# Token-wise queries, keys and values for cross attention, and a state space block in two parts around the normed output's transposes

## The reference

```
def gated_rmsnorm(y, z, w):                       # after each group's scan
    u = y * silu(z); ug = u in 8 groups of 256
    return ug * rsqrt(mean(ug * ug) + EPS) * w

def memory_cross_attention(h, mem_n, ...):
    q = rmsnorm_2((h @ wq_x).reshape(S, 4, 128), xq_norm_g)
    kv = (mem_n @ wkv_x).reshape(256, 2, 4, 128)
    k = rmsnorm_2(kv[:, 0], xk_norm_g); v = kv[:, 1]
    p = softmax(q k^T * 128 ** -0.5)
    return (p v).reshape(S, 512) @ wo_x
```

## Time and profile before

| | |
|---|---|
| median of 3 runs | 1980.33 us (1977.35 to 1981.42) |
| the profiled execution's own time | 1978.49 us |
| its span | 1976.8 us |
| state space stage | about 97 to 481 us of the span, some 50 us a group |
| cross attention, first key panel to first scores | 1491.3 to 1562.97 us |
| PE busy | 96% of the span |

### The profile page before, as it was taken

The page is one execution under the profiler, slowest core; times in us unless marked ns, Lnnn a source line. Parts: engine busy times, 40 slices in busy tenths (PEclk is TensorE's granted clock), DMA queues, the critical chain, the costliest instruction groups (busy, mean ns, idle before and its releaser), DMA issues.

```text
span 1976.8 us, 26607 instructions
## 1 busy us (share of the span) xinstructions
PE 1900.3 (96%) x9819; PEld 1601.9 (81%) x9819; DVE 851.5 (43%) x1696; ACT 712.0 (36%) x1334; POOL 1458.1 (74%) x1307
## 2 busy tenths in 40 slices
PE   6999999999999999989999999898999989999998
PEld 4888888887887888878888888797678878888887
DVE  3666666663004443545501421637661354302411
ACT  4466666655014665123101210467643332101200
POOL 6799888789865446988988988653436358888984
PEclk9999999999999999989999999899999899999999
DMA  7322122222342222322333233222023112333331
GB/s 212 97 61 63 59 63 65 64 65 64 107 123 65 75 60 86 129 85 64 106 86 106 85 107 88 71 71 65 30 66 129 54 42 87 100 92 100 91 107 64
DMA packets 213069, 165.71 MB, mean 84 GB/s; under 512 B 14446, under 2 KB 209329, under 8 KB 212578
## 3 DMA queue, kind: packets, MB, share of 16 engines
q1 hardware_dynamic: 207286, 147.35, 25.4%
q10 hardware_dynamic: 5676, 16.95, 2.5%
HBM read 161.11 MB, written 7.37 MB: 85 GB/s over the span
## 4 chain that ended last, share of the span: by engine, by line
PE 80%; POOL 9%; DVE 4%; ACT 3%; issue 2%; PEld 2%; PEldq 0%; DMA 0%; DVEq 0%; SPq 0%; ACTq 0%; POOLq 0%
PE bank L391 57%; PE bank L438 6%; POOL w_lo L2755 4%; PE bank L410 4%; PE bank L1389 3%; PE bank L1365 2%; POOL w_hi L2747 2%; PEld bank L391 2%; PE bank L1375 1%; POOL arena L1067 1%; PE bank L1049 1%; PE bank L1027 1%; PE bank L484 1%; ACT w_hi L1220 1%; PE bank L998 1%
## 5 line engine op out<-in xcount | busy, mean ns | idle before, releaser
L2755 POOL TENSOR_TENSOR w_lo<-w_raw,w_hi 128x512 fp32r<-128x512 f32 (+2 forms) x590 | 733.9, 1275 | 123.1 <-ACT w_hi L1220 115.7
L2747 POOL TENSOR_TENSOR w_hi<-w_raw,one 128x512 fp32r<-128x512 f32 (+1 forms) x452 | 459.8, 1048 | 312.8 <-PE bank L391 270.8
L391 PE MATMUL bank<-h_hi,w_hi 128*128 128x512 f32 (+1 forms) x1056 | 418.3, 396 | 10.6 <-POOL w_lo L2755 6.5
L391 PE MATMUL bank<-h_hi,w_lo 128*128 128x512 f32 (+1 forms) x1056 | 407.5, 386 | 0.0
L391 PE MATMUL bank<-h_lo,w_hi 128*128 128x512 f32 (+1 forms) x1056 | 406.8, 385 | 0.0
L391 PE MATMUL bank<-a_hi,w_hi 128*128 128x512 f32 x848 | 331.1, 390 | 3.3 <-DVEq L353 1.6
L391 PE MATMUL bank<-a_hi,w_lo 128*128 128x512 f32 x848 | 330.0, 389 | 0.0
L391 PE MATMUL bank<-a_lo,w_hi 128*128 128x512 f32 x848 | 330.0, 389 | 0.0
L391 PEld LDWEIGHTS bank<-h_hi,w_hi 128*128 128x128 f32 x1056 | 200.5, 190 | 49.5 <-POOL w_lo L2755 7.4
L391 PEld LDWEIGHTS bank<-h_hi,w_lo 128*128 128x128 f32 x1056 | 200.0, 189 | 40.4
L391 PEld LDWEIGHTS bank<-h_lo,w_hi 128*128 128x128 f32 x1056 | 200.7, 190 | 35.2
(11 more groups left out here) (428 smaller groups left out, 2824.6 us busy)
## 6 DMA issues: line engine op xcount, KB each, us to landing
w_raw<-in_w_ff SPq DMA_DIRECT2D x32, 1024.0 KB, 5.5
w_raw<-in_w_in SPq DMA_DIRECT2D x31, 1024.0 KB, 5.4
w_raw<-in_w_mlp_in SPq DMA_DIRECT2D x16, 1024.0 KB, 5.3
w_raw<-in_w_mlp_out SPq DMA_DIRECT2D x16, 1024.0 KB, 5.6
w_raw<-in_w_in SPq DMA_DIRECT2D x26, 512.0 KB, 4.6
w_raw<-in_w_ssd_out SPq DMA_DIRECT2D x8, 1024.0 KB, 5.7
bias_rows<-bias_row ACTq DMA_DIRECT2D x1, 4096.0 KB, 15.7
w_raw<-in_w_attn_out SPq DMA_DIRECT2D x4, 1024.0 KB, 5.1
```

What stands on the lines that cost most here:

```text
L391: mm = pe.matmul(bank[:, 0:ntok], a, b[:, koff + k, 0:ntok], start=(k == 0 and n == 0), stop=(k == L.kb - 1 and n == 2))
L2747: pool.tensor_tensor(w_hi[:, slot, part], raw[:, slot, part], one[:].broadcast_to([P, n]), ALU.mult).then_inc(split_hi, 1)
L2755: ins = pool.tensor_tensor(w_lo[:, slot, part], raw[:, slot, part], w_hi[:, slot, part].bitcast(F32), ALU.subtract)
```

## The change

**State space.** `ssd_block_pe` takes a range of contraction slices. In chunk 0 of groups 1 to 7 PE issues slices 0 to 2 of block 2 (9 matmuls), then the wait for `st_done`, the transposes, and slices 3 to 7 (15 matmuls). Other engines' lists stay as they are.

**Cross attention.** `L_kvx` is cut into `L_kx` and `L_vx`, two panels each, and the order of panels becomes keys, queries, values. All three are made token-wise: `memory_panel_pe` for keys and values, `pe_panel_tokens` for queries. The sum of squares of a head is then along the free dimension: ACT copies and squares (`key_act`, `query_act`), DVE reduces (`tensor_reduce`), ACT takes the root, and DVE takes the reciprocal and multiplies in place. The scale of x's norm is a value per partition now, and goes into ACT's copies. PE turns keys and queries to features (8 transposes for the keys, twice 8 for the queries, in `cross_turn_pe`) and ACT copies them out with the gains (`query_turned_act`). Values need no turn. `sums_pe`, `rows_pe`, `scale_dve` and the copy of the norm's row (L678) go; the norm's row itself (`root_row_pe`) stays.

```diff
@@ -308,8 +308,10 @@
         L_ukv = Linear(1, 1, 1024, [0] * 2 * T, lambda i: rows_of(io["w_ukv_2"][0]))
         L_gate_m.append(Linear(1, DB, 256, [0, 128], column_panels(w_in2, 1280, 1)))
         L_out2 = full(io["w_out_2"][0], D)
-        L_kvx = full(io["wkv_x_2"][0], D)
+        wkv_x = rows_of(io["wkv_x_2"][0])
+        L_kx = Linear(2, DB, 256, [0], column_panels(wkv_x, 0, 2))
         L_qx = full(io["wq_x_2"][0], 512)
+        L_vx = Linear(2, DB, 256, [0], column_panels(wkv_x, 512, 2))
         wo_x = rows_of(io["wo_x_2"][0])
         L_ox = Linear(2, 4, 512, [0, 128, 256, 384], column_panels(wo_x, 0, 2, 512))
         L_mlp.append(mlp_linears(io["w_ff1_2"][0], io["w_ff2_2"][0]))
...
@@ -675,7 +676,8 @@
         def unscaled_root_dve(dve, gain):
             if gain in ("mix2", "norm_x"):
                 root_dve(dve)
-                dve_link(dve.tensor_copy(NORM_ROW[gain], NROW[:]))
+                if gain == "mix2":
+                    dve_link(dve.tensor_copy(RROW, NROW[:]))
             else:
                 square_root_dve(dve)
...
@@ -1190,11 +1195,14 @@
                 states_pe(pe, g)
                 for c in range(T):
                     chunk_scores_pe(pe, g, c)
-                    if g and c == 0:
-                        pe.wait_ge(st_done, 3 * g + 3)
-                        gnorm_pe(pe, g - 1)
                     for b in PE_BLOCKS[c]:
-                        ssd_block_pe(pe, g + 1, b)
+                        if g and c == 0:
+                            ssd_block_pe(pe, g + 1, b, range(0, 3))
+                            pe.wait_ge(st_done, 3 * g + 3)
+                            gnorm_pe(pe, g - 1)
+                            ssd_block_pe(pe, g + 1, b, range(3, DB))
+                        else:
+                            ssd_block_pe(pe, g + 1, b)
                     chunk_out_pe(pe, g, c)
...
-            for i in range(L_kvx.n):
-                pe_panel(pe, L_kvx, i, i, h_x, ntok=N_MEM)
-                if i == 0:
-                    root_sum_pe(pe)
-                if i == 1:
-                    root_row_pe(pe)
-            pe_panel_rows(pe, L_qx, 0, a_upper_x, normed("norm_x"))
-            pe_panel(pe, L_qx, 1, 1, a_upper_x)
-            for h in range(X_HEADS):
-                pe.wait_ge(la["sq"], h + 1)
-                sums_pe(pe, CROSS_ITEMS[h][0], [SQX[:, h, :]], tiles=X_TILES)
-            pe.wait_ge(acc_free, L_qx.b0 + 1)
-            for b in range(4):
-                if b >= 2:
-                    pe.wait_ge(xa_vt, b - 1)
-                for t in range(X_TILES):
-                    mm = pe.transpose(banks[5 + b % 2][:, t * P:(t + 1) * P], XVT[:, b, t * P:(t + 1) * P], ident[:])
-                mm.then_inc(xa_v, 1)
-            for h in range(X_HEADS):
-                pe.wait_ge(la["sq"], X_HEADS + h + 1)
-                sums_pe(pe, CROSS_ITEMS[X_HEADS + h][0], [SQX[:, h, :]])
-            pe.wait_ge(xa_vt, 4)
-            for i, (_, tiles) in enumerate(CROSS_ITEMS):
-                rows_pe(pe, i, tiles)
-            pe.wait_ge(xa_q, 1)
+            memory_panel_pe(pe, L_kx, 0)
+            root_sum_pe(pe)
+            memory_panel_pe(pe, L_kx, 1)
+            root_row_pe(pe)
+            pe.wait_ge(nx_lo, NORM_AT["norm_x"] + DB)
+            pe_panel_tokens(pe, L_qx, 0, 0, a_upper_x, only=0)
+            pe.wait_ge(xk_scaled, 2)
+            for i in range(2):
+                for h in range(2):
+                    for t in range(X_TILES):
+                        c = (2 * i + h) * P
+                        mm = pe.transpose(banks[6 + i][:, (2 * h + t) * P:(2 * h + t + 1) * P], XKT[:, t, c:c + P], ident[:])
+                mm.then_inc(xk_turned, 1)
+            pe_panel_tokens(pe, L_qx, 0, 0, a_upper_x, only=1)
+            for j in range(2):
+                pe_panel_tokens(pe, L_qx, 1, 1, a_upper_x, only=j)
+            cross_turn_pe(pe, 0)
+            memory_panel_pe(pe, L_vx, 0)
+            cross_turn_pe(pe, 1)
+            memory_panel_pe(pe, L_vx, 1)
+            pe.wait_ge(xk_kept, 2)
+            pe.wait_ge(xq_kept, 2)
             attn_pe(pe, cross_units(), XMEM)
             pe.wait_ge(at_out, at_base["pe"])
             pe_to_features(pe, XO, T, 4)
 
-        def kvx_act(act, b):
-            act.wait_ge(acc_ready, L_kvx.b0 + b + 1)
-            dst = XK[:, b, :] if b < X_HEADS else XVT[:, b - X_HEADS, :]
-            act.activation(dst, acc(L_kvx, b, 0, P, N_MEM), ACT.Copy).then_inc(acc_free, 1)
+        def memory_panel_pe(pe, L, i):
+
+            slot, blk = (L.p0 + i) % 2, L.b0 + i
+            pe.wait_ge(split_ready, L.p0 + i + 1)
+            pe.wait_ge(acc_free, blk - 3)
+            for t in range(X_TILES):
+                tok = slice(t * P, (t + 1) * P)
+                for k in range(L.kb):
+                    wh, wl = (w[:, slot, k * L.w:(k + 1) * L.w] for w in (w_hi, w_lo))
+                    for n, (a, b) in enumerate(((h_hi, wh), (h_lo, wh), (h_hi, wl))):
+                        mm = pe.matmul(banks[blk % 4][:, t * L.w:(t + 1) * L.w], a[:, k, tok], b,
+                                       start=(k == 0 and n == 0), stop=(k == L.kb - 1 and n == 2))
+            mm.then_inc(acc_ready, 1)
+
+        def cross_turn_pe(pe, i):
+
+            pe.wait_ge(xq_scaled, i + 1)
+            if i:
+                pe.wait_ge(xk_kept, 2)
+            for h in range(2):
+                for t in range(T):
+                    c = (2 * i + h) * P
+                    mm = pe.transpose(banks[4 + 2 * i + h][:, t * P:(t + 1) * P], XQT[:, t, c:c + P], ident[:])
+            mm.then_inc(xq_turned, 1)
+
+        def key_act(act, i):
+            bank = acc(L_kx, i)
+            act.wait_ge(acc_ready, L_kx.b0 + i + 1)
+            act.activation(XKT[:, :, i * 256:(i + 1) * 256], bank.rearrange("p (t f) -> p t f", t=X_TILES), ACT.Copy)
+            act.activation(K_SQ[i], bank, ACT.Square).then_inc(acc_free, 1)
+
+        def query_act(act, i, j):
+            b = 2 * i + j
+            act.wait_ge(acc_ready, L_qx.b0 + b + 1)
+            for t in range(2):
+                row, src = 2 * j + t, acc(L_qx, b)[:, t * 256:(t + 1) * 256]
+                act.activation(XQT[:, row, i * 256:(i + 1) * 256], src, ACT.Copy, scale=nstat[:, row:row + 1])
+                ins = act.activation(Q_SQ[b][:, t * 256:(t + 1) * 256], src, ACT.Square, scale=nstat[:, row:row + 1])
+            ins.then_inc(acc_free, 1)
+
+        def query_root_act(act, i):
+            act.wait_ge(xq_red, 2 * i + 2)
+            act.activation(lstat[:, 8 + 8 * i:16 + 8 * i], lstat[:, 8 + 8 * i:16 + 8 * i], ACT.Sqrt, scale=1.0 / X_HD, bias=eps_col).then_inc(xq_root, 1)
+
+        def query_turned_act(act, i):
+            act.wait_ge(xq_turned, i + 1)
+            for h in range(2):
+                ins = act.activation(XQ[:, 2 * i + h, :], banks[4 + 2 * i + h][:], ACT.Copy, scale=colv("xq"))
+            ins.then_inc(xq_kept, 1)
+
+        def value_act(act, i):
+            act.wait_ge(acc_ready, L_vx.b0 + i + 1)
+            act.activation(XV[:, :, i * 256:(i + 1) * 256], acc(L_vx, i).rearrange("p (t f) -> p t f", t=X_TILES), ACT.Copy).then_inc(acc_free, 1)
...
             root_act(act)
-            for b in range(DB):
-                kvx_act(act, b)
-                if b % 2:
-                    split_high_act(act, *((L_kvx, 2), (L_kvx, 3), (L_qx, 0), (L_qx, 1))[b // 2])
+            for i in range(2):
+                key_act(act, i)
+                split_high_act(act, L_qx, i)
+            act.wait_ge(xk_red, 2)
+            act.activation(lstat[:, 0:8], lstat[:, 0:8], ACT.Sqrt, scale=1.0 / X_HD, bias=eps_col).then_inc(xk_root, 1)
             act.wait_ge(nx_inverse, nx_n["root"])
-            for h in range(X_HEADS):
-                act.activation(SQX[:, h, 0:N_MEM], XK[:, h, :], ACT.Square).then_inc(la["sq"], 1)
-            for h in range(X_HEADS):
-                act.wait_ge(acc_free, L_qx.b0 + h + 1)
-                act.wait_ge(la["sum"], h + 1)
-                act.activation(SQX[:, h, :], XQ[:, h, :], ACT.Square).then_inc(la["sq"], 1)
-            for b in range(4):
-                act.wait_ge(xa_v, b + 1)
-                act.activation(XV[:, :, b * P:(b + 1) * P], banks[5 + b % 2][:, 0:N_MEM].rearrange("p (t f) -> p t f", t=X_TILES),
-                               ACT.Copy).then_inc(xa_vt, 1)
-            act.wait_ge(la["sum"], 2 * X_HEADS)
-            act.activation(lstat[:, 0:cross_cols], SUM_BANK[:, 0:cross_cols], ACT.Sqrt, scale=1.0 / X_HD, bias=eps_col).then_inc(la["root"], 1)
+            query_act(act, 0, 0)
+            for i in range(2):
+                act.wait_ge(xk_turned, i + 1)
+                act.activation(XK[:, 2 * i:2 * i + 2, :], banks[6 + i][:].rearrange("p (h s) -> p h s", h=2), ACT.Copy, scale=colv("xk")).then_inc(xk_kept, 1)
+            query_act(act, 0, 1)
+            split_high_act(act, L_vx, 0)
+            query_root_act(act, 0)
+            query_act(act, 1, 0)
+            query_act(act, 1, 1)
```

(62 more changed lines are left out.)

26 lines of the change are left out of this document (14 added, 12 removed).

## The result

The changed kernel took **1961.67 us** (median of 4 runs, 1959.1 to 1962.5) beside 1979.65 us for the kernel before (median of 4 runs, 1977.35 to 1981.42). The ratio is 0.9911, interval 0.9898 to 0.9924, so the gain is 18.0 us, between 15.0 and 20.2. I had predicted 1957.5 us and a gain of 22.6. The profiled execution took 1961.56 us, 16.9 less than that of before (1978.49).

What follows compares the result with a forecast made beforehand. PE, busy 96% of the span, was taken to bound the kernel by its own list, waits and slow stretches. Gains of 8.1 (groups) and 14.5 us (cross attention) gave 22.6, hence 1957.5 us; range 1952 to 1966.

Steps and rivals of the forecast that it cites:

- The transposes' waits are filled: State space groups: nine matmuls, 2.05 us, run ahead of each wait, the longest 1.64 us, so each is filled.
- So POOL's cycle moves with PE from group to group: State space groups: POOL's 4.39 us idle was a wait for ACT, which waits for PE's transposes; a group lasts 49.1 us.
- The term of 8.1 us: State space groups: gain from seven removed waits, 8.30 us less 0.22 coming back in group 7; ends 0 and 8.3.
- the slack of chunk 3: State space groups: PE's product needing DVE's sum had 2.49 us of slack, and 0.85 after the change: enough.
- the wait in the groups is only moved: State space groups, rival: PE is held at each chunk's output instead; their gain 0, total 14.5, 1965.8 us; chance 0.09.
- The sum said 39.6 us: Cross attention: from the norm's row to the first scores 39.6 us instead of 54.1, a gain of 14.5.
- The wait before value panel 1: Cross attention: PE waits 1.8 us there for POOL's low part, ends 0.6 and 2.1.
- the second wait: Cross attention: PE waits at most 0.8 us for the second query half's multiplication, inside the wait for value panel 1.
- DVE's multiplication: Cross attention: multiplying a query half, 128x1024 elements in SBUF, while POOL works, was estimated at 1.24 us.
- The keys' wait: Cross attention: waiting for the keys' multiplication when query block 0 ends, 0 to 0.5 us, taken as net 0.
- The clock rival: Cross attention: the gap before value panel 1 costs clock too, 1.74 us; gain 20.8, 1959.5 us; chance 0.14.
- no second wait over 1 us: Cross attention, sign: a second wait above 1 us between the query blocks would show the prediction wrong.

Runs made afterwards that it cites:

- the second and third profiles: The changed kernel profiled twice more, unedited; 1956.97 and 1957.97 us, one run each.
- e4: The changed kernel with ACT's high part of key panel 1 made ahead of the last block's two activations; 1959.55 us, ratio 0.9902.
- e5: The changed kernel with 14 more matmuls, their result unread, in PE's gap before value panel 1; 1960.2 us, ratio 0.9906.
- e6: The changed kernel with DVE's multiplication of each query half cut to 128 of 1024 columns; 1960.04 us, ratio 0.9906.

## Why the prediction was right, and where it was not

**The direction and the range** were right; the size was 4.6 us too large by the medians, and one step failed. The range of 14 us was wide enough to hold that. By its steps:

**The transposes' waits are filled: right.** All seven are gone, by nine matmuls, and none comes back.

**"So POOL's cycle moves with PE from group to group": this step failed.** The term of 8.1 us measures 5.0: from the second group's states to the last group's 306.1 us passed before (132.52 to 438.60) and 301.1 after (134.06 to 435.12). A group is 49.80 us, not 49.1. The prediction saw POOL's idle time of 4.39 us before the panel, and ACT ahead of it, and took it that ACT waits for PE's transposes. It waits for POOL itself, by way of DVE's sum, the convolution and `silu`. The first link stood in its own rows: DVE's sum waited 0.58 us for POOL's mask. I checked the slack of chunk 3 against POOL's masks at their present times only (0.85 us), and these times move with the ring. The kernel before had the evidence. Three starts of POOL's cycle there, from its timeline:

```profile
126.84 5.04 POOL L2755 TENSOR_TENSOR w_lo<-w_raw,w_hi 128x512 fp32r<-128x512 f32 x4 [4.39 <-PE bank L391]
...
176.63 5.04 POOL L2755 TENSOR_TENSOR w_lo<-w_raw,w_hi 128x512 fp32r<-128x512 f32 x4 [4.39 <-ACT w_hi L1220]
...
226.42 5.02 POOL L2755 TENSOR_TENSOR w_lo<-w_raw,w_hi 128x512 fp32r<-128x512 f32 x4 [4.39 <-ACT w_hi L1220]
```

They are 49.79 us apart, while PE's groups were 50.79 apart. POOL was already running on a ring of its own, faster than PE, and was using up its slack. Only from the third of these cycles on did it idle a second time in each, 0.6 to 1.0 us before its second panel (first at 240.37), and its period grew to 50.4 and 50.8. So the floor of 49.8 could be read before the change: PE could gain 1.0 a group and no more. The rival that fits is "the wait in the groups is only moved"; it came true for 3.1 of the 8.1 us, through POOL, and with a gain of 5 instead of 0.

**The cross attention: right to 0.2 us.** The sum said 39.6 us from the norm's row to the scores; the second and third profiles have 39.77 each, the first 41.27. Against 54.11 that is a gain of 14.34 where 14.5 stood. The wait before value panel 1 was put at 1.8 us; measured are 1.26, and 0.6 before the transposes ahead of it, for DVE's multiplication, 1.9 together. The prediction had the second wait inside the first, and it lies in front of it, but POOL's end sets the sum in both. DVE's multiplication was put at 1.24 us and took 2.18, POOL's part at 5.03 + 1.2 and took 5.97. The keys' wait came out at 0, as taken, but by luck: beside POOL DVE's two multiplications took 3.25 us, not 1.4, and ended at 1511.10, when query block 0 ended at 1511.11. Nothing is in hand there.

**The clock rival** (the gap before value panel 1 costs clock too) happened in one of three profiles of the changed kernel, at 1.5 us where 1.74 was written, and in e4 alone among the six experiments that leave a gap there. It is neither excluded nor the cause of a fixed loss. I had not foreseen that key panel 1 and the block near the start vary in the same way, by 1.0 and 1.4 to 1.6 us.

**Nothing else was late.** From the first scores to the start of the last matmul of values the 16 units took 23.3 us (23.5 before), and no second wait over 1 us stands between the query blocks.

**The sum again.** 5.0 and 14.3 make 19.3 us, inside the measured 15.0 to 20.2. The 1.3 between this and the medians' 18.0 is less than the 3.9 us by which the clock alone set two executions of the changed kernel apart. Had the ring been seen, the prediction would have been 1957.5 + 3.1 = 1960.6.

## What to carry to other kernels

Before counting a PE wait as gain in every iteration, look for a ring of other engines: measure the period of each helper engine from its own repeating row, over the first iterations, where it may still run at its own pace. A helper whose period is shorter than PE's by less than the wait that you remove is the next bound, whatever its slack at one place looks like. And an in-order queue closes such rings by neighbourhood alone: here one activation, moved ahead of an instruction it had nothing to do with, was worth 4.3 us in the groups, where the block in two parts had given 5.0.

## What was not expected of the hardware

- The clock fell or not at the same place of the same program: 7.51 or 6.01 us for the same 48 matmuls behind the same 1.26 us of idle, with 1.4 to 1.6 us near the start as well. Two profiles of one kernel differed by 3.9 us for this alone, of 4.5 in all.
- A panel of 48 took 6.01 us behind an idle PE (repeat of the change) and 5.76 behind a busy one (e5), both at granted clock 1.00.
- DVE's multiplication of 128x1024 took 2.18 us beside POOL, and one of 128x128 still 1.25 (e6).
